# Score products of two attention steps and of two query tiles issued in pairs, in a one-core decoder layer

## The reference, cut to what matters

```python
h = rms_norm(x, pre_mix_gain[layer]) * (1.0 + scale_m) + shift_m
...
s = jnp.einsum("bqhmd,bkhmd->bhmqk", qb, kb).astype(jnp.float32) * scale
p = jax.nn.softmax(s + bias[None, :, None], axis=-1)
pd = p[:, :, 0] - lam * p[:, :, 1]
...
sol = lax.linalg.triangular_solve(L, rhs, left_side=True, lower=True, unit_diagonal=True)
...
q = (xb @ w_query).reshape(P, PEER_HEADS, 2, PEER_HALF)
s = jnp.einsum("phcd,hcnd->phcn", q, sub_keys)
s_top, i_top = lax.top_k(s, K)
```

## Time and profile before

| | us |
|---|---|
| median of 3 runs | 1651.88 (1651.84 to 1651.9) |
| the profiled execution | 1652.03 |
| its span, first to last instruction | 1650.2 |
| TensorE busy | 1639.7 (99%) |
| VectorE busy | 1177.1 (71%) |
| GpSimd busy | 912.1 (55%) |
| ScalarE busy | 685.3 (42%) |

### The profile page before, as it was taken

How to read it: one execution, slowest core, us unless ns; L and a number is a source line. 1 busy time by engine, 2 the same in 40 slices (tenths; PEclk the granted TensorE clock), 3 DMA queues, 4 the chain that set the end, 5 groups by cost and what they waited for, 6 DMA issues and landing times.

```text
span 1650.2 us, 24985 instructions
## 1 busy us (share of the span) xinstructions
PE 1639.7 (99%) x7732; PEld 1358.6 (82%) x7732; DVE 1177.1 (71%) x2972; ACT 685.3 (42%) x1035; POOL 912.1 (55%) x724
## 2 busy tenths in 40 slices
PE   8999999999999999999999999999999999999998
PEld 7777889888888888888888888888888888888887
DVE  7877675556887987768776722225888888888886
ACT  6446655633422344443434434333333333333333
POOL 0232243243656666676666766745676766777730
PEclk9999999999999999999999999999999999999999
DMA  9999032232354554444444445667999999999994
GB/s 365 343 409 396 25 92 89 91 128 90 116 171 161 172 172 154 151 137 146 140 153 146 141 153 177 187 204 263 340 378 356 361 391 340 371 381 356 378 342 158
DMA packets 156628, 376.39 MB, mean 228 GB/s; under 512 B 37521, under 2 KB 72849, under 8 KB 153362
## 3 DMA queue, kind: packets, MB, share of 16 engines
q1 hardware_dynamic: 119026, 308.08, 52.6%
q0 software_dynamic: 34816, 67.41, 11.5%
q10 hardware_dynamic: 2720, 0.16, 0.1%
HBM read 312.06 MB, written 63.50 MB: 228 GB/s over the span
## 4 chain that ended last, share of the span: by engine, by line
PE 98%; DMA 0%; DVE 0%; SPq 0%; ACT 0%; issue 0%; DVEq 0%; ACTq 0%
PE bank L1328 18%; PE bank L1329 18%; PE bank L1330 18%; PE bank L1870 11%; PE bank L1868 11%; PE bank L1866 11%; PE bank L1806 1%; PE bank L1440 1%; PE bank L1470 1%; DMA raw<-in_in_tiles 0%; PE bank L1756 0%; PE bank L1757 0%; PE bank L1758 0%; PE bank L1777 0%; PE bank L1339 0%; PE bank L1776 0%
## 5 line engine op out<-in xcount | busy, mean ns | idle before, releaser
L788 POOL DMA_INDIRECT gate_scratch<-merged,idx_cell x384 | 428.0, 1115 | 204.8 <-issue 108.6
L1328 PE MATMUL bank<-act_hi,whi 128*128 128x512 f32 x1296 | 507.9, 392 | 0.0
L1329 PE MATMUL bank<-act_lo,whi 128*128 128x512 f32 x1296 | 504.8, 389 | 0.0
L1330 PE MATMUL bank<-act_hi,wlo 128*128 128x512 f32 x1296 | 504.8, 389 | 0.0
L2357 DVE TENSOR_TENSOR wlo<-raw,whi 128x1024 fp32r<-128x1024 f32 x247 | 302.0, 1223 | 226.2 <-ACT whi L1234 224.3
L1868 PE MATMUL bank<-wlo,chi 128*128 128x512 f32 x768 | 299.0, 389 | 0.0
L1870 PE MATMUL bank<-whi,clo 128*128 128x512 f32 x768 | 299.0, 389 | 0.0
L1866 PE MATMUL bank<-whi,chi 128*128 128x512 f32 x768 | 299.0, 389 | 0.0
L1330 PEld LDWEIGHTS bank<-act_hi,wlo 128*128 128x128 f32 x1296 | 243.4, 188 | 50.7
L1328 PEld LDWEIGHTS bank<-act_hi,whi 128*128 128x128 f32 x1296 | 243.6, 188 | 49.4
L1329 PEld LDWEIGHTS bank<-act_lo,whi 128*128 128x128 f32 x1296 | 243.5, 188 | 49.2
(11 more groups left out here) (412 smaller groups left out, 1747.0 us busy)
## 6 DMA issues: line engine op xcount, KB each, us to landing
raw<-in_expert_tiles SPq DMA_DIRECT2D x256, 512.0 KB, 3.7
act_scratch<-aout SPq DMA_DIRECT2D x128, 256.0 KB, 2.2
gate_scratch<-vbeta SPq DMA_DIRECT2D x24, 1024.0 KB, 18.3
a_in<-act_scratch SPq DMA_DIRECT2D x128, 192.0 KB, 6.4
g_in<-gate_scratch SPq DMA_DIRECT2D x128, 192.0 KB
raw<-in_in_tiles SPq DMA_DIRECT2D x28, 512.0 KB, 12.9
modr<-in_mod_tiles SPq DMA_DIRECT2D x24, 512.0 KB, 10.6
raw<-in_query_tiles SPq DMA_DIRECT2D x16, 512.0 KB, 4.3
```

The source lines that it names most:

```text
L788: g.indirect_dma_start(out=gate_cells, out_offset=bass.IndirectOffsetOnAxis(ap=idx_cell[:, b, k:k + 1], axis=0), in_=merged[:, b, k:k + 1] ...
L1328: mm(out_bank[:], whi[:, slot, w], act_hi[:, k, :], start=(k == 0), stop=False)
L1329: mm(out_bank[:], whi[:, slot, w], act_lo[:, k, :], start=False, stop=False)
L1330: last = mm(out_bank[:], wlo[:, slot, w], act_hi[:, k, :], start=False, stop=(k == KD - 1))
```

## The change

- Attention: the scores of steps s and s + 1 are both issued at even s; odd steps issue none.
- Query tiles: key products n - 2 and n - 1 are both issued behind tile n for even n (n = 16 stands for the end); odd n issue none. ScalarE's loop is as it was.
- Block inverses, second level: two products instead of four, each with the 128 weight columns and the 128 moving columns of two heads; the two halves of the diagonal of the 128 x 128 result are used, and ScalarE's copy takes them from there.
- Start: VectorE's low part of row 0 of h comes behind the sums of modulation rows 2 and 3 and the coefficients of column 1.

```diff
                     for odd in range(2):
                         rows = slice(odd * CJ, (odd + 1) * CJ)
                         pair = PM[rows, t, H * CJ:2 * H * CJ].rearrange("p (q two n) -> p q two n", q=2, two=2)
-                        last = sc.copy(pair[:, :, odd, :],
-                                       bank[t % 2][rows, 0:2 * CJ].rearrange("p (q n) -> p q n", q=2))
+                        made = bank[t % 2][rows, 0:H * CJ].rearrange("p (q two n) -> p q two n", q=2, two=2)
+                        last = sc.copy(pair[:, :, odd, :], made[:, :, odd, :])
...
-                if s < H * NB:
+                if s < H * NB and s % 2 == 0:
                     scores(s)
+                    scores(s + 1)
...
-                for h in range(H):
-                    even = side(Tm[:, t, hs(h)], k, 0)
-                    if n < NB:
-                        last = mm(bank[t % 2][0:CJ, cj(h)], LMA[:, t, cj(h)], even, start=True, stop=True)
-                    else:
-                        rows = slice(h % 2 * CJ, (h % 2 + 1) * CJ)
-                        last = mm(bank[t % 2][rows, cj(h // 2)], LM[:, t, cj(h)], even, start=True, stop=True)
+                if n < NB:
+                    for h in range(H):
+                        last = mm(bank[t % 2][0:CJ, cj(h)], LMA[:, t, cj(h)], side(Tm[:, t, hs(h)], k, 0),
+                                  start=True, stop=True)
+                else:
+                    for q in range(2):
+                        last = mm(bank[t % 2][:, hs(q)], LM[:, t, hs(q)],
+                                  side(Tm[:, t, q * 2 * HD:(q + 1) * 2 * HD], k, 0), start=True, stop=True)
...
-                for m in range(2) if n == 2 else (n - 1,):
-                    key_scores(m)
+                if n % 2 == 0:
+                    key_scores(n - 2)
+                    key_scores(n - 1)
...
             weight_low(0)
-            low(0, 0, wk)
             mod_tile(2)
             mod_tile(3)
             mod_columns(0, 1, 2)
+            low(0, 0, wk)
             mod_tile(4)
```

## The result

The changed kernel takes 1680.52 us (median of 5, 1678.91 to 1681.11) against 1651.88 us: a ratio of 1.0167, 95% interval 1.0156 to 1.0178. The forecast was 1670.0 us in a range of 1667 to 1677: the direction and the place are right, the size is not. The profiled execution took 1680.73 us, with a span of 1678.9.

The account below looks back on a forecast made before the run. TensorE's own stream was taken as the bound, with no waits for weights. Terms +20.9 (stalls), -2.2 (scores), +0.1 (P) and -0.7 (start) sum to +18.1 us, giving 1670.0 us against the median, range 1667 to 1677.

Parts of the forecast that it names:

- Which edit decides, and through which queue: Query tiles: paired key products make ScalarE cast weights late, so TensorE stalls six times 3.49 us, +20.9 us.
- the gains: Other three edits: scores -2.2, P +0.1, first low part of h -0.7 us.
- Pairing key products saves nothing: Query stage: a pair takes 1.70 us, two separate blocks about 1.6 to 1.8, so 0.0 us saved on TensorE.
- Scores: Attention: paired score blocks save the second block's entry and non-streaming time, -2.2 us (-2.4 to -0.7).
- the row of loads: Attention trace, step 3: four weight loads issued within 0.30 us of the block's start, while its first products stream.
- P: Block inverses, second level: two 128-column products for four of 64 columns, +0.1 us (-0.3 to +0.5).
- Low part of h: Start: low part behind two modulation rows lets column 1 come earlier, -0.7 us (-0.9 to 0.0).
- the clock behind the stalls: Query stage, rival: half clock after each stall, up to 33 us more, 1670 to 1703 us; chance 0.10.
- a gap of 1.28 us: Start of the old trace: TensorE's wait for column 1, next four products at full rate; cited against the half-clock rival.
- the 3.05 us gap at the start: Kernel's start: TensorE without work, then products at half rate or held by their diagonals; six 3.5 us stalls called closer.
- 1681 if a third of a tile is slowed: Query stage, half-clock rival (chance 0.10): total of 1681 us if a third of a tile runs slow after each stall.
- the 10 and 20 there: Kernel's start: TensorE read as running 10 products in 8 to 10 us and 20 in 12 to 14 us.

Follow-up runs that it names:

- filled kernel: Changed kernel with 15 idle identity products on TensorE behind each of the six key-product pairs it stands still after: 1669.45 us.
- P alone: Kernel before with only the block-inverse edit, second-level products P of two heads in one product: 1652.02 us against 1652.00, ratio 0.9998.
- the kernel with 7 products: Changed kernel with 7 idle identity products on TensorE behind each of the six key-product pairs it stands still after: 1668.77 us.

## Why the prediction was wrong

- **Which edit decides, and through which queue: right.** The cast behind the copy in ScalarE's list, six odd tiles, 3.41 us each (forecast 3.49), 20.5 us (20.9). The filled kernel measures that term alone: 1669.45 us, 0.5 us from the forecast, which had only this term and the gains.
- **Pairing key products saves nothing: right** (12.68 us for two tiles and a pair).
- **Scores: right,** -2.5 (-2.2), with the loads of the second block hidden, as the row of loads had said.
- **P: right in that it is worth nothing,** 0.0 in the medians (+0.1), 0.2 us more in the trace of P alone. The longer products are there (0.89 for 0.61 us on the first two blocks, 1.5 times and not twice), and ScalarE's copies hide only a part of them.
- **Low part of h: right in mechanism, its size not settled.** Forecast -0.7; natural tile 2 starts 0.95 us earlier with this edit alone, 0.7 us earlier with the old order of the key products (29.27 for 29.96), and the medians, -0.45, are not told apart from no change. In the profile after it is only -0.3: there TensorE waited 0.7 us for a diagonal, its first product of h came 2.0 us later (18.77 for 16.78), and so the table of waits holds no wait for the low part.
- **The step that failed: the clock behind the stalls.** The sum put it at nothing: its +20.9 us holds only the time in which TensorE stands still. The products behind it at half rate were a rival, with a chance of 0.10 and bounds of 0 and 33 us. What spoke for nothing was the full rate behind a gap of 1.28 us, though the prediction itself called stalls of 3.5 us closer to the 3.05 us gap at the start; by its own reading the term belonged in the sum. In its place the runs showed 11.1 us, the part that filling the stalls took back. The periods of the changed kernel, from 349.69, 367.45, 385.17, 402.89, 421.90 and 439.65 to 451.94 us, lie 1.6 (five times) and 2.9 us (once) above what the wait alone makes (16.11 us, and for the last, with one tile, 10.69 in the kernel with 7 products): 11.0 us. The prediction's "1681 if a third of a tile is slowed" came near the 1680.5 measured, but the third was worked out from no row, so that is luck. Nor did any run show what held the products at the start: the granted clock reads 1.00 in both rows, and the 10 and 20 there are instructions, two to a product.
The Trainium skill (TensorE: Matmul & The Clock Gate, HAM oscillation) describes such a loop, groups of products between waits (there for DMA) that each send the clock to half. The trace agrees in six places of six, at 0.50 or 0.51.
- **The range.** Its upper end, 1677, took in a small part of the rival. A cost that the nearer of two rows speaks for belongs in the range with the whole size given for it, here 11 us, whatever its chance.

Sum by the runs: 20.5 + 11.1 - 2.5 + 0.0 - 0.5 = +28.6 us; measured +28.6.

## What to carry to other kernels

Before moving an instruction of one engine to batch it, walk through the other engines' lists for what stands behind the wait for it: here a copy that came later held a weight cast that had nothing to do with it, and the cast moved ahead of that copy, in ScalarE's list, is worth 31.8 us. And price a new stall of TensorE twice, the time it stands and the products behind it; filling the stall with idle products gives the second part back (11 us here), removing it gives back both. Batch products where a block has an entry to save (64-row scores, 0.29 us each), not where blocks follow their neighbours without one (key products, 0.0).

## What the runs showed of the hardware

- Six gaps of 1.6 us each between dense products left the granted clock at full. Of six of 2.5 us three lowered it; all six of 3.15 us did, in the changed kernel and again with the pairs alone. A fall showed in the products behind the gap and cost 1.6 us in most places, 1.3 to 2.9 in all of them: 2.9 where about 14 products stood 0.43 us apart (from 408.58 us), 1.6 where it was about 8.
- The clock can fall without a gap. In the profiled execution with the low part alone it was lower in step 14 of the attention, behind scores of 64 rows, two transposes and 8 products of a single column (16 instructions, L1479; 182.2 to 185.0 us), with no wait of TensorE there:

```profile
184.00:186.00 2.00, 2.00 (x15) 1.86 (x15) 1.76 (x5) 1.75 (x7) 1.80 (x1) 0.88 0.00 0
186.00:188.00 2.00, 2.00 (x6) 1.55 (x5) 1.85 (x6) 2.00 (x9) 0.00 (x0) 0.50 0.00 0
```

The products of the column tile behind it stand 0.43 us apart, and 1.6 us are lost there. The profiled execution of P alone, 1653.55 us, has the same lower stretch (0.50 from 186 to 188 us); that of before has not (1.00), with the same work in step 14. What sets it off wasn't tried and stays open.
